# A two-layer hybrid decoder trunk: the mixer's order of weight splits and level matmuls, and a narrower standing operand

## The reference

```python
z = h @ w_in                      # 1024 -> 3088 columns: rq rk rv rg gq gk gv ga gg
ro = retention(rope(rq), rope(rk) / 8, rv)               # 4 heads, fixed decay
log_a = log_sigmoid(ga @ w_a2 + b_a2) / 16               # per token and key dimension
go = gla(gq / 8, gk, gv, log_a)                          # S_t = diag(a_t) S_(t-1) + k_t v_t; o_t = q_t S_t
out = concat(norm(ro) * silu(rg), norm(go) * silu(gg)) @ w_out
```

## Time and profile before

| | us |
|---|---|
| median of 3 runs | 1184.18 (1184.04 to 1184.34) |
| the profiled execution, its time | 1184.15 |
| its span, first to last instruction | 1182.1 |
| PE busy | 1172.7 (99%) |
| DVE busy | 841.4 (71%) |
| ACT busy | 702.6 (59%) |
| POOL busy | 150.4 (13%) |

### The profile page before, as it was taken

How to read it: one execution, slowest core, us unless ns; L and a number is a source line. 1 busy time by engine, 2 the same in 40 slices (tenths; PEclk the granted TensorE clock), 3 DMA queues, 4 the chain that set the end, 5 groups by cost and what they waited for, 6 DMA issues and landing times. The chain is left out here.

```text
span 1182.1 us, 17336 instructions
## 1 busy us (share of the span) xinstructions
PE 1172.7 (99%) x6164; PEld 997.3 (84%) x6164; DVE 841.4 (71%) x1300; ACT 702.6 (59%) x1225; POOL 150.4 (13%) x220
## 2 busy tenths in 40 slices
PE   9999999999999999999999999999999999999998
PEld 7888888788888888888888888887888888888886
DVE  6866656888767678775487875479887676777752
ACT  7655545756666557654476764376567565666641
POOL 3000002573100100000000000036431001000000
PEclk9999999999999999999999999999999999999999
DMA  9756554454545365555465555554545454555540
GB/s 358 271 184 235 194 202 160 175 179 143 195 144 178 131 204 199 178 201 209 142 214 193 198 196 196 196 201 138 179 154 185 144 177 146 202 187 183 201 168 35
DMA packets 33411, 217.92 MB, mean 184 GB/s; under 512 B 3952, under 2 KB 4208, under 8 KB 9792
## 3 DMA queue, kind: packets, MB, share of 16 engines
q1 hardware_dynamic: 33200, 216.90, 53.7%
q10 hardware_dynamic: 144, 0.13, 0.0%
HBM read 215.97 MB, written 1.05 MB: 184 GB/s over the span
## 5 line engine op out<-in xcount | busy, mean ns | idle before, releaser
L1539 DVE SCALAR_TENSOR_TENSOR w_lo<-raw,first,w_hi 128x512 fp32r<-128x512 f32 x576 | 417.2, 779 | 81.4 <-ACT w_hi L1089 80.2
L1089 ACT ACTIVATE w_hi<-raw,first 128x512 fp32r<-128x512 f32 x568 | 369.1, 716 | 90.3 <-PE acc L761 47.0
L760 PE MATMUL acc<-xT,w_hi 128*128 128x512 f32 x864 | 300.2, 391 | 0.0
L761 PE MATMUL acc<-xT,w_lo 128*128 128x256 f32 x864 | 241.9, 280 | 0.0
L585 PE MATMUL acc<-w_hi,xT 128*128 128x512 f32 x576 | 227.4, 395 | 0.0
L589 PE MATMUL acc<-w_lo,xT 128*128 128x512 f32 x576 | 224.6, 390 | 0.7 <-DVE w_lo L1539 0.7
L586 PE MATMUL acc<-w_hi,xT 128*128 128x512 f32 x576 | 224.4, 390 | 0.0
L760 PEld LDWEIGHTS acc<-xT,w_hi 128*128 128x128 f32 x864 | 161.6, 187 | 35.4
L1531 DVE TENSOR_TENSOR w_lo<-raw,w_hi 128x1024 fp32r<-128x1024 f32 x112 | 124.6, 1146 | 87.5 <-ACT w_hi L1083 87.2
L761 PEld LDWEIGHTS acc<-xT,w_lo 128*128 128x128 f32 x864 | 163.3, 189 | 0.1
L1083 ACT ACTIVATE w_hi<-raw 128x1024 fp32r<-128x1024 f32 x112 | 106.6, 991 | 92.2 <-PE acc L589 75.5
(11 more groups left out here) (219 smaller groups left out, 1377.8 us busy)
## 6 DMA issues: line engine op xcount, KB each, us to landing
raw<-in_gu SPq DMA_DIRECT2D x86, 1024.0 KB, 5.1
raw<-in_down SPq DMA_DIRECT2D x32, 1024.0 KB, 4.8
raw<-in_in SPq DMA_DIRECT2D x24, 1024.0 KB, 5.1
raw<-in_kv SPq DMA_DIRECT2D x16, 1024.0 KB, 5.2
raw<-in_down SPq DMA_DIRECT2D x16, 768.0 KB, 4.2
raw<-in_out SPq DMA_DIRECT2D x8, 1024.0 KB, 5.1
raw<-in_q SPq DMA_DIRECT2D x8, 1024.0 KB, 5.1
raw<-in_o SPq DMA_DIRECT2D x8, 1024.0 KB, 5.1
```

The costliest lines, as they stand in the source:

```text
L760: pe.matmul(o[:, :], w_hi[:, slot, kk, c:c + P], xT[:, :, k, :], start=k == 0, stop=False)
L761: mm = pe.matmul(o[:, TOK:2 * TOK], w_lo[:, slot, kk, c:c + P], xT_hi[:, k, :], start=False, stop=k == KD - 1)
L1089: act.activation(w_hi[:, slot, k, :], raw[:, slot, k, :], ACT.Copy, scale=gains[:, ds(g, 1)]).then_inc(s_hi, 1)
L1539: dve.scalar_tensor_tensor(w_lo[:, slot, k, :], raw[:, slot, k, :], gains[:, ds(g, 1)], w_hi[:, slot, k, :].bitcast(F32), ALU.mult, ALU.su ...
```

## The change

It makes four edits, in both layers.

1. DVE: the low splits of the first two blocks of (C_IN+1, second half) go ahead of `x_norm(l, 1, 1)`, the other two stay behind it. PE: the transposes of tile 1 go ahead of block 6 of pass 1, not of block 5.
2. PE: `second_keys` (retention scores of the second tile, and level 0) runs behind pass 5, not half way through it; level 1 runs half way through pass 6, not behind pass 5. The order among them is the same.
3. DVE: the low splits of the first two blocks of (C_IN+3, second half) go ahead of `retention_mask(1)` and `level_out(0)`, the other two stay behind these.
4. For the level of 64 tokens the standing operand is the first 64 columns of the tile, and the result 64 rows of the bank. DVE takes these out by a plain copy of 64 rows without the mask (and without the nop ahead of it).

```diff
--- before.py
+++ after.py
@@ -834,7 +834,8 @@
                             tile = A[rows, r, t * P:(t + 1) * P]
                             later = tile.rearrange("p (g two b) -> p g two b", two=2, b=b)[:, :, 1, :]
                             c = c0 + (2 * t + r) * 64
-                            mm = pe.matmul(mb[e][:, c:c + 64], tile, later, start=True, stop=True)
+                            keys = 64 if b == 64 else P
+                            mm = pe.matmul(mb[e][0:keys, c:c + 64], tile[:, 0:keys], later, start=True, stop=True)
                             if last and t == TT - 1 and r == 1:
                                 mm.then_inc(s_m[e], 1)
 
@@ -940,7 +941,7 @@
                     return wait
 
                 def second_tile(ks):
-                    if ks == 5:
+                    if ks == 6:
                         x_transposes(l, 1, 1)
                 pair(l, C_IN, (Q_IN, Q_IN + 1), (xT_hi, xT_lo),
                      before_k={0: x_split(0), 1: second_tile, 2: x_split(1)}, before_last=low_rank)
@@ -949,9 +950,9 @@
                 def second_keys():
                     retention_scores(1)
                     level(l, 0, False, True)
-                inside = {4: {4: gqk_transposes}, 5: {4: second_keys}, 7: {4: lambda: levels(l, 2)},
+                inside = {4: {4: gqk_transposes}, 6: {4: lambda: level(l, 1, True, True)}, 7: {4: lambda: levels(l, 2)},
                           8: {4: lambda: levels(l, 4)}, 9: {4: lambda: levels(l, 6)}, 10: {4: retention_outputs}}
-                behind = {4: lambda: retention_scores(0), 5: lambda: level(l, 1, True, True), 10: gated_outputs,
+                behind = {4: lambda: retention_scores(0), 5: second_keys, 10: gated_outputs,
                           11: lambda: mixed_transposes(l, 0)}
                 for n in range(4, 12):
                     c, t = n // 2, n % 2
@@ -1766,6 +1767,9 @@
                             dve.wait_ge(s_mf[e], m_no(l, LV_USE[n]))
                         dst = pg[:, e].rearrange("p c (g two b) -> p c g two b", two=2, b=b)[:, :, :, 1, :]
                         src = mb[e][:, c0:c0 + 4 * 64].rearrange("p (c g b) -> p c g b", c=4, b=b)
+                        if b == 64:
+                            dve.tensor_copy(dst[0:64, :, 0, :], src[0:64, :, 0, :]).then_inc(s_mf[e], 1)
+                            continue
                         msk = lv_mask[:, n - 1, :].rearrange("p (g b) -> p g b", b=b)
                         msk = msk.unsqueeze(1).to_broadcast([P, 4, 64 // b, b])
 
@@ -1809,8 +1813,9 @@
                     s = (slice(None), t, slice(g * COL, (g + 1) * COL))
                     dve.tensor_tensor(o_sb[s], o_sb[s], gate[s], ALU.mult).then_inc(s_mixed, 1)
 
+                split_lo(l, C_IN + 1, 1, ks=(0, 1))
                 x_norm(l, 1, 1)
-                split_lo(l, C_IN + 1, 1)
+                split_lo(l, C_IN + 1, 1, ks=(2, 3))
                 x_lo(l, 1, 1)
                 split_lo(l, C_IN + 2, 0)
 
@@ -1854,9 +1859,10 @@
                     d = qk_dot[:, :].rearrange("p (c e) -> p c e", e=2)[:, :, e:e + 1].to_broadcast([P, 4, P])
                     dve.tensor_tensor(pg[:, e], ident[:, :].unsqueeze(1).to_broadcast([P, 4, P]), d,
                                       ALU.mult).then_inc(s_pg, 1)
+                split_lo(l, C_IN + 3, 1, ks=(0, 1))
                 retention_mask(1)
                 level_out(0)
-                split_after(4)
+                split_lo(l, C_IN + 3, 1, ks=(2, 3))
                 level_out(1)
                 split_after(5)
                 split_after(6)
```

## The result

The changed kernel takes 1191.74 us (median of 6 runs, 1191.37 to 1192.93), the kernel before in the same comparison 1184.26 (1184.04 to 1184.71): ratio 1.0064, 95% interval 1.0051 to 1.0077, so 7.5 us slower. The forecast was 1181.5. The profiled execution is the one of 1191.39, its span 1189.3.

The account below looks back on a forecast made before the run. PE was taken to bound the kernel, busy 1172.7 of 1182.1 us. PE's gains of 2.92, capped by POOL at 2.84, less 0.2 for contention, gave 2.6: 1184.15 - 2.6 = 1181.5, range 1180.4 to 1183.0.

Parts of the forecast that it names:

- The sign: Whole kernel: faster than before, below 1181.81 us, at chance 0.58; within the measurement's resolution 0.37; slower 0.05.
- edit 4: Level 1's narrower loads on PE: at most 0.43 us per layer, +0.25 taken; DVE's copy of 64 rows: nothing.
- the pricing of contention: POOL's multiplies beside DVE: 1.17 us beside splits, 0.73 beside mask and copy; worst case 0.9 more per layer.
- Edit 1: PE's stall in pass 1 and late transposes go: 0.68 us in the first layer, 0.54 in the second.
- Edit 2: PE's stall at level 0 goes, as level 0 runs half a pass later: 0.85 us per layer.
- Edit 3: DVE's two splits fill its wait before the mask; level 1's bank ready 0.3 us early; POOL contention counted as even.
- the pause of 0.71: POOL's wait at decayed(4) for a buffer used by PE's levels 2, 3; earlier levels would free 0.71 us.
- Rival (a): POOL contention uneven: decayed 1 costs 0.9 us more per layer, exponents 3 give nothing back; 1183.1, half 1182.2; chance 0.28.
- Rival (d): Level 1 on PE: 64 x 64 standing operand stops loads running ahead, +6.4 us per layer, 1194; chance 0.04.
- The cap by POOL: POOL's chain of levels limits the gain to 1.49 us in the first layer, 1.35 in the second, 2.84 together.
- The slack behind decayed 5: Between POOL's decayed(5) ending and PE needing it for level 5: 0.10 us after a semaphore.
- the shift of 0.68: POOL's chain of levels starts earlier by PE's gain in pass 1: 0.68 us in layer 0, 0.54 in layer 1.

Follow-up runs that it names:

- the version with shifted copies: Changed kernel with two more small DVE copies (64 rows x 100 columns) among level 1's plain copies, so the splits begin later; 1193.38 us.

## Why the prediction was wrong

**The sign** failed at one sentence, at the end of edit 4: DVE's copy of 64 rows "has 256 elements per row as before: nothing". Its own duration was indeed unchanged (0.74), and so the term was right as it was meant. What it did was to change how the burst behind it shares with POOL, and that cost 6.16 in one layer and about 5.2 in the other. The step that lets this through is the pricing of contention by the worst row seen, 1.17 against 0.73. The runs show that as a price of taking turns; the other case, being shut out for the whole burst (5.76 to 6.16), was in no row of before, and no bound from both sides was put on it.

The Trainium skill (SBUF — State Buffer, Who interferes with whom) says that VectorE and GpSimd share a pair of ports, that an instruction of VectorE with two SBUF inputs contends with one of GpSimd that reads SBUF, and that the pair is an exclusive lock for which the order of issue decides who blocks. The trace agrees with the contention. The rest it can test only by the starts in the profile, which need not be the moments at which an engine takes the ports, and POOL's are rough: in the changed kernel POOL's multiply started at 236.74, ahead of the burst at 236.86, and lost eight splits in a row. If starts were issues, the multiply would have gone first by that rule, or waited for one split of 0.67. Nor does the rule tell why, at distances equal to 0.01, the engines took turns behind 128 rows and did not behind 96 or 64.

**The clock** was not in the sum. A wait of PE was priced at its length. In the changed kernel 3.5 of waiting in the first layer came with 2.65 of slower clock. The runs show when it does not: with copies of 64 rows added in the kernel before, PE waited 3.7 in two waits, the granted clock stayed at 1.00, and the loss was 3.7; with 96 rows it waited less, 3.0, but lost 6.8, the clock being 0.69 from 832 to 843.

**Edit 1** was right in its place: transposes at 202.01 against a forecast of 202.06, no stall. PE gained 0.68. The norm's delay, put at 1.2 to 1.4, is 201.2 - 200.26 = 0.94 by the prediction's own rows, and it was 0.75 (201.01); nothing hung on it. POOL's chain of levels started only 0.53 earlier (226.39 before; 226.24 in the version with the masked copy of 128 rows, whose profiled execution runs 0.38 late from before the first edit on).

**Edit 2** was right: 231.43 for a forecast 231.5, no wait, 0.87 gained (1.41 down to 0.54) against 0.85, and another 0.09 in the return to the pass (231.97 to 232.52 is 0.55, before 0.64).

**Edit 3** was right in its places: bank of level 1 free in time (`level_out(0)` 233.85 + 0.74 = 234.6, forecast 235.2, wanted at 235.47), and contention moved but even. From the start of decayed 1 to the end of decayed 5 POOL took 19.51 before (232.81 to 252.32) and 18.81 in the version with the masked copy of 128 rows (233.12 to 251.93); the difference is the pause of 0.71 and no more. That it is even was luck: decayed 1's first multiply became dearer as feared (1.19 for 0.74), exponents 3 gave nothing back (1.08 and 1.09 for 0.94 and 1.09), and what did was decayed 2's first multiply (0.73 for 1.19), of which the prediction says nothing. Rival (a) as put, with decayed 1 dearer and nothing given back, did not come.

**Edit 4** on PE was sized too low: 1.04 down to 0.61, 0.43, the upper bound. I took 0.25 on the ground that the matmul and not the load would limit. PE's row of the changed kernel by line, load (ns minimum/median/maximum):
```profile
L838 PEld LDWEIGHTS mb<-gqk x224: 129/188/335, 235.5 to 852.6; 64*128 64x128 f32 x96, 64*64 64x64 f32 x16
```
The Trainium skill (TensorE: Matmul & The Clock Gate, Wait — 56ns, not 53.3ns?) has a floor of about 62 ns per matmul with one kind of decoding, quoted in the prediction as the case in which this edit is worth nothing. Sixteen in 0.61 are 0.038 each: the floor is not there. Rival (d) had the sign and, by accident, the size (1194), but its mechanism, loads that stop running ahead, is refuted by the same row and by the run in which the matmuls are untouched and the loss is all there.

**The cap by POOL** was the right limit and was set too high. With the lock-out away, PE waits for POOL at levels 4, 5 and for 0.22 at levels 2, 3:
```profile
243.51 1.11 PE L838 MATMUL mb<-gqk 64*128 64x64 f32 x16 [0.22 <-POOL gqk L2204]
...
251.99 1.11 PE L838 MATMUL mb<-gqk 64*128 64x64 f32 x16 [0.64 <-POOL gqk L2204]
```
The slack behind decayed 5 was 0.09 (forecast 0.10), the pause gave its 0.70. What failed is the shift of 0.68 ahead of it: 0.15 was lost before POOL's chain began, and 0.46 in its first 6.4 us, since an exponent there went from 0.63 to 1.07.
```profile
227.16 0.62 POOL L2190 TENSOR_TENSOR o_sb<-cum 128x256 f32<-128x256 f32 x1
227.73 1.07 POOL L2191 TENSOR_TENSOR o_sb<-cum 128x256 f32<-128x256 f32 x1
```
DVE's two splits now start there at 227.58, ahead of that exponent; before, at 227.87, they came level with it (227.88). The prediction looked for contention where edit 3 moves splits and not where edit 1 moves DVE against POOL. By decayed 1 the chain is 0.07 ahead instead of 0.68. So PE's level 5 comes 0.07 + 0.70 + 0.09 = 0.86 earlier; about 0.1 of that goes into PE's restart behind the wait, and the first layer gains 0.72. In the second PE is 0.56 ahead when the mixer begins and 1.20 at levels 6, a gain of 0.64. Together 1.4 by starts, of the forecast 2.6, and 1.7 by the medians. (Between the layers PE comes forward by another 0.2, in steps of 0.05; the kernel before with added copies of 128 rows, which has none of the edits, does so too.) The time of that version, 1182.5, is where rival (a) had put half its price (1182.2), for another reason.

One chance was added up loosely: three quarters of the forecast's 0.47 are 0.35, not 0.37, so faster had 0.56.

Left open: why the number of rows of an operation decides how later ones share with POOL; why the version with shifted copies locked out a burst later; whether it is the source or the size that makes the small copy harmless; and whether the rows count where they are read (PSUM) or where they are written (SBUF), which every copy had alike. The rows are shown to be the cause, by three pairs with equal timing in which nothing else differs: the kernel before with 128 and 96 rows, the changed kernel's masked copy with 128 and 64, the added copies with 128 and 64. What in the chip ties them to the ports is not shown.

## What to carry to other kernels

When VectorE runs a series of instructions with two SBUF inputs beside GpSimd work that something waits for, keep the copies out of PSUM just ahead of it at the full 128 rows, even where half are masked out. That rests on this one kernel: shortening them saved nothing in their own time (0.74 either way) and cost 6 to 9 us where it met the wrong distance, and copies of 64 rows added beside full ones cost 3.7. After any change around such a series look for one GpSimd operation many times its usual length and for splits at their undisturbed pace; the loser's row, and not the winner's, shows the cause. And give contention a bound that is the length of the whole burst, not the dearest single row of the trace.

## What the runs showed of the hardware that was not expected

- An operation of GpSimd can be shut out for a whole burst of VectorE's: 3.1 and 3.4 for four splits, 5.7 to 6.2 for eight, against 0.6 to 1.2 in turns. It ends about 0.5 behind the last split before VectorE pauses, and a start that the profile shows 0.12 to 0.25 ahead of the burst does not protect it.
- It hangs on the rows (64 or 96, not 128) of a copy out of PSUM one or two operations earlier, and on GpSimd's start between 0.25 ahead of the burst's and 0.10 behind it; one second burst stands outside this and is unexplained. No-operations do not break it, nor does a full-height copy of 8 columns.
- In the changed kernel two waits of PE of 1.73 and 1.58 with 1.1 of matmuls between came with the clock at 1.2 GHz for 6.8 us in the first layer, and two like them for 3.4 us in the second. In other runs a single wait of 1.85 left it at 2.4 GHz in both layers, and one of 1.52 did so in the first layer and not in the second (0.66 to 0.69): the length of the wait alone doesn't tell.
- Matmuls of 64 rows x 64 standing columns x 64 run at 0.038 us each with their loads; with 128 standing columns 32 take 2.0, 0.063 each.
